# A hybrid mixer and expert block on one Trainium2 core: running sums of the decays through DRAM, tokens first in stage 1

## The chip, the core and the metric

The program runs on one core of one Trainium2 chip. The core has five engines with a queue of instructions each: TensorE (PE in the views), VectorE (DVE), ScalarE (ACT), GpSimd (POOL) and SyncE (SP, which here only issues transfers), and 16 DMA engines. The engines wait for one another on semaphores only. The metric is device time in microseconds of one execution: the median of three runs.

## What is computed

One block over 256 tokens of width 1024, float32 throughout: a modulated norm, a hybrid mixer (a gated delta rule, "gdn", with 8 heads, beside a state-space part, "ssd", with 16 heads), and a mixture of 32 experts; then a second block of other kind. The change touches the head of the first mixer:

```
mod = silu(c) @ ada_w + ada_b                      # six rows of 1024
h = rmsnorm(x, norm1_g) * (1 + sc1) + sh1
proj = h @ w_in                                    # qkv and gate of gdn; gate, xbc and dt of ssd
qkv = silu(causal_dwconv(gdn_qkv)); q, k = l2norm(q) * DK**-0.5, l2norm(k)
g  = -exp(gdn_a_log) * softplus(gdn_a + gdn_dt_bias)     # log decays, gdn
xbc = silu(causal_dwconv(ssd_xbc) + conv_b)
a  = -exp(ssd_a_log) * softplus(ssd_dt + ssd_dt_bias)    # log decays, ssd
gam = cumsum(g); a_cum = cumsum(a)                 # over the tokens of a chunk
decay = exp(gam[l] - gam[s]) for s <= l, per head  # the same for a_cum
```

Both parts need, for every head and every pair of tokens, the difference of two running sums. The kernel has tokens on the 128 partitions, in two halves (T = 2), so the sum of token l is a column (one value per partition) and that of token s a row that must stand on all partitions.

## The kernel before

Each `with nc.Block()` is a stage: all engines meet at its end, and within it each engine's code is an order written out by hand. The first four hold the first mixer.

*Stage 1* (L331 to L552): SP loads `c`, `ada_b` and `norm1_g` as rows, the tokens `x_res`, and through a ring of six slots of 2 MB the chunks of `ada_w` and `w_in` (`Ring.add`, `Ring.load`, `Ring.take`: a chunk's load waits for the semaphore that its slot's last user raises). TensorE multiplies the condition with four chunks of `ada_w` (L299, `modulation_sums`), ScalarE copies the result (L479), and `spread` (L398) brings it to columns. ScalarE squares the tokens (L489), takes the root (L491), VectorE scales the tokens (L523), TensorE transposes them (L420), and VectorE applies shift and scale feature block by feature block (L538, `s_hk`). Then TensorE computes the 12 projection units of `xbc` (L406, `half_unit`, four feature blocks of eight at a time), VectorE runs the convolution of each unit (L322, L324: four instructions), TensorE the narrow products (L454: the decays' inputs) and the ssd gates (L463).

*Stage 2* (L604 to L842): 24 units of gdn projection (L629, 8 products each) from six chunks of `w_in`, each with VectorE's convolution (L320, L324) and ScalarE's silu (L736). PSUM has three banks for units: unit u waits until the convolution of unit u - 3 is done. Between the units lies the ssd part for half t at units 0, 3, 5, 9 (and 12 on): `decay_rows` (L653) multiplies the decays, repeated by ScalarE along the free dimension (L708), with the triangle `tri_le`, which gives the running sums as rows on all partitions; VectorE's `pair_exponents` (L781) subtracts the column and writes `dmat`; ScalarE exponentiates (L717). `lengths(b)` (L639) sums squares of q and k for the norm and waits for ScalarE's copy of the one before (L754). At the end TensorE computes four gdn gates (L701).

*Stage 3* (L1202 to L1740): the chunked delta rule. ScalarE repeats the gdn decays (L1485); TensorE's `decay_rows` (L1258) and `decay_columns` (L1263) put the differences in PSUM; ScalarE takes the absolute value (L1491) and exponentiates (L1493); VectorE's `lower` (L1571) makes the triangular matrix, GpSimd masks it (L1227), and the inverse is built in levels (L1331, L1347, L1353), beside which modulation chunks, the output projection and their loads run. SP loads `mods` (`ada_b` on all partitions, L1207) here. At its end the first expert weights are loaded as slots come free.

*After it*: the first experts stream 32 sets of weights from DRAM through eight slots (L1805, L1832), each load waiting for the product that frees its slot; then the second mixer and second experts.

## Time and profile before

| | us |
|---|---|
| median of three runs | 2095.73 (2095.64 to 2097.11) |
| profiled execution | 2094.25 |
| its span | 2092.5 |
| TensorE busy in the span | 1936.1 (93%) |
| VectorE, ScalarE, GpSimd busy | 499.9, 325.9, 81.9 |
| DMA | 707.29 MB, 338 GB/s over the span |

The span runs from the first to the last instruction of the profiled execution; the rest of its time lies around it. TensorE's matmuls are pipelined and float32 ones leave two records each; "busy" includes the tail of each group. "idle before" is the time in which the engine had nothing to run ahead of a row, with what ended it. PEclk is the granted TensorE clock, as a share of full speed.

### The profile page before, as it was taken

How to read it: one execution, taken by the hardware profiler on the slowest of the kernel's cores; microseconds unless marked ns; L12 is line 12 of the kernel's file. 1: busy time of each engine (PE TensorE's matmuls, PEld its weight loads, DVE VectorE, ACT ScalarE, POOL GpSimd, SP SyncE). 2: the span in 40 equal slices, each digit the busy share in tenths (PEclk: the TensorE clock that was granted, in tenths of full speed). 3: DMA queues.
4: the chain of work that ended last, by engine and by line, in shares of the span. 5: the costliest groups of instructions: out<-in, count | busy, mean ns of one | idle time of the engine just before them, and what ended most of it. 6: DMA issues, size and time to landing. Idle time of an engine off the chain costs nothing. (4 is left out here: it accounts for less than half of the span.)

```text
span 2092.5 us, 24721 instructions
## 1 busy us (share of the span) xinstructions
PE 1936.1 (93%) x10246; PEld 907.1 (43%) x10246; DVE 499.9 (24%) x1040; ACT 325.9 (16%) x580; POOL 81.9 (4%) x185
## 2 busy tenths in 40 slices
PE   6999999989999999999999999999999887877877
PEld 4687665543333333333333333445454432322332
DVE  1456444422222122121112221232342200000000
ACT  2234421210000000000000000124341100000001
POOL 2010031000000000000000000000020000000000
PEclk9999999999999999999999999999999999999999
DMA  9333157599999999999999999955255799999996
GB/s 339 128 131 108 62 208 291 218 374 421 428 428 428 428 428 428 429 428 429 429 428 429 428 429 428 407 166 174 64 201 205 331 425 428 427 429 428 429 428 273
DMA packets 99150, 707.29 MB, mean 338 GB/s; under 512 B 12378, under 2 KB 17996, under 8 KB 61836
## 3 DMA queue, kind: packets, MB, share of 16 engines
q1 hardware_dynamic: 99084, 706.36, 82.1%
q8 instruction: 47, 0.77, 0.1%
q14 instruction: 19, 0.16, 0.0%
HBM read 705.29 MB, written 1.05 MB: 338 GB/s over the span
## 5 line engine op out<-in xcount | busy, mean ns | idle before, releaser
L1805 PE MATMUL ps<-ring,arena 128*64 128x512 f32 x1536 | 337.9, 593 | 11.2 <-DMA ring<-in_moe_w_gu 11.2
L3049 PE MATMUL ps<-ring,arena 128*32 128x512 f32 x768 | 176.8, 630 | 46.6 <-DMA ring<-in_w_up 24.1
L1805 PEld LDWEIGHTS ps<-ring,arena 128*64 128x64 f32 x1536 | 109.9, 137 | 233.0 <-issue 206.7
L1832 PE MATMUL ps<-ring,arena 128*64 128x512 f32 x768 | 170.2, 592 | 0.0
L2265 PE MATMUL ps<-ring 128*128 128x512 f32 (+1 forms) x320 | 138.6, 583 | 0.7 <-ACT ring L2658 0.6
L1862 ACT ACTIVATE arena<-arena 128x512 f32<-128x512 f32 x32 | 20.1, 630 | 758.3 <-DVE arena L1893 758.3
L3049 PEld LDWEIGHTS ps<-ring,arena 128*32 128x32 f32 x768 | 52.0, 115 | 170.5 <-issue 166.7
L1805 PE MATMUL ps<-arena 128*64 128x512 f32 x512 | 114.0, 593 | 4.1 <-DMA arena<-in_moe_w_gu 4.1
L1168 PEld LDWEIGHTS ps<-arena 128*128 128x128 f32 x832 | 100.1, 198 | 35.3 <-issue 32.7
L1168 PE MATMUL ps<-arena 128*128 128x128 f32 x832 | 108.1, 287 | 2.3 <-DVE arena L1160 1.3
L1832 PEld LDWEIGHTS ps<-ring,arena 128*64 128x64 f32 x768 | 54.9, 137 | 109.9 <-issue 96.1
L1893 DVE TENSOR_SCALAR arena<-ps 128x512 f32<-128x512 f32 x32 | 22.1, 692 | 316.3 <-PE ps L1805 316.3
L2265 PEld LDWEIGHTS ps<-ring 128*128 128x128 f32 x320 | 59.3, 191 | 66.5 <-issue 64.1
L629 PE MATMUL ps<-arena,ring 128*128 128x256 f32 x384 | 85.1, 379 | 1.0 <-PEq L331 1.0
L629 PEld LDWEIGHTS ps<-arena,ring 128*128 128x128 f32 x384 | 72.7, 190 | 15.3 <-issue 6.1
L1904 DVE TENSOR_TENSOR arena<-ps,arena 128x512 f32<-128x512 f32 x32 | 22.1, 692 | 237.2 <-PE ps L1832 237.2
L3070 PE MATMUL ps<-ring,arena 128*32 128x512 f32 x384 | 63.4, 652 | 13.7 <-DMA ring<-in_w_down 13.7
L1805 PEld LDWEIGHTS ps<-arena 128*64 128x64 f32 x512 | 36.3, 137 | 78.6 <-issue 69.2
L3049 PE MATMUL ps<-arena 128*32 128x512 f32 x256 | 56.5, 593 | 13.6 <-DMA arena<-in_w_up 7.2
L3122 DVE TENSOR_TENSOR arena<-arena 128x256 f32<-128x256 f32 x8 | 3.4, 426 | 271.2 <-PE ps L3049 271.2
L1776 PE MATMUL ps<-arena 64*128 64x512 f32 x264 | 65.6, 615 | 0.9 <-DVE arena L1904 0.9
L1794 PE MATMUL ps<-arena,masks 128*64 128x512 f32 x256 | 60.4, 592 | 1.3 <-issue 1.3
(608 smaller groups left out, 1980.9 us busy)
## 6 DMA issues: line engine op xcount, KB each, us to landing
ring<-in_moe_w_gu SPq DMA_DIRECT2D x96, 2048.0 KB, 28.0
ring<-in_moe_w_down SPq DMA_DIRECT2D x48, 2048.0 KB, 30.2
arena<-in_moe_w_gu SPq DMA_DIRECT2D x31, 2048.0 KB, 26.7
ring<-in_w_gate SPq DMA_DIRECT2D x26, 2048.0 KB, 26.9
ring<-in_w_down SPq DMA_DIRECT2D x24, 2048.0 KB, 27.1
ring<-in_w_in SPq DMA_DIRECT2D x22, 2048.0 KB, 8.5
ring<-in_w_up SPq DMA_DIRECT2D x22, 2048.0 KB, 24.1
arena<-in_moe_w_down SPq DMA_DIRECT2D x16, 2048.0 KB, 32.2
```

The costliest lines, as they stand in the source:

```text
L629: last = M.matmul(ps[:, u % GB, 0:T * P], w[:, k, c * P:(c + 1) * P], hT[:, k, :], start=(k == 0), stop=(k == KD - 1))
L1168: last = M.matmul(ps[:, bank, k4 * P:(k4 + 1) * P], x_tok[:, t, k * P:(k + 1) * P], onehot[:, t, :], start=(t == 0), stop=(t == T - 1))
L1776: last = M.matmul(ps[:, 2 * t + j, :], GT[halves[j], t, :], y2[halves[j], :], start=False, stop=False, skip_group_check=True)
L1794: M.matmul(ps[halves[j], 4 + which, :], bsel[ee][:, 2 * which + j, :], bias_all, start=True, stop=False)
L1805: last = M.matmul(ps[halves[j], 4 + which, :], xgT[buf][:, k, CAP * ee:CAP * ee + CAP], w[k2][:, at:at + 512], start=False, stop=(k == KD ...
L1832: last = M.matmul(ps[halves[j], 6, :], yT[:, k % KH, halves[k // KH]], w[k % KH][:, 512 * j:512 * j + 512], start=False, stop=(k == 2 * KH ...
L1862: A.activation(sg, tg, ACT.Sigmoid, scale=1.702).then_inc(s_sig, 1)
L1893: V.tensor_scalar(tg, ps[:, 4, :], 7.0, None, ALU.min).then_inc(s_g, 1)
L1904: V.tensor_tensor(y2, ps[:, 6, :], g2s, ALU.mult).then_inc(s_y2, 1)
L2265: last = M.matmul(ps[:, bank, 0:n], uT[:, k, t * P:(t + 1) * P], w[:, k, :], start=(k == 0), stop=(k == KD - 1))
L3049: last = M.matmul(ps[quads[e], 4 + which, :], xgT[:, k, quads[e]], w[e][k], start=(k == 0), stop=(k == KD - 1))
L3070: last = M.matmul(ps[quads[e], (4, 7)[d], :], yT[:, k, quads[e]], w[e][k][:, 512 * d:512 * (d + 1)], start=(k == 0), stop=(k == KH - 1))
```

## The change

Four things are changed.

1. *Running sums through DRAM.* TensorE multiplies the decays of all 24 heads (8 gdn, 16 ssd) with `tri_le` once per half, which gives the sums with heads on 24 partitions; ScalarE copies them; SP stores them to a DRAM tensor `decay_sums` and loads them back repeated on all 128 partitions: `abc` for the ssd part (again for the second half once the products have read it), `gbc` for the gdn part. `decay_rows` of both stages, `decay_columns` of stage 3 and ScalarE's repeats go. VectorE's `pair_exponents` of the first eight heads stands at units 2 and 14 instead of 0 and 12. In stage 3 ScalarE computes the absolute differences itself, head by head.
2. *Lengths one unit later*: `lengths` at even units 6 to 20 instead of odd units 5 to 19.
3. *Tokens first in stage 1*: `x` is loaded first; the raw tokens are transposed; the root factors are spread over partitions by a product with a diagonal and multiplied in as VectorE takes the transposes from PSUM.
4. *`xbc` weights by rows*: four chunks of 256 rows by 1536 columns in place of three of 1024 by 512, and the 12 units take feature blocks 0 to 3 first, all of them, then 4 to 7. The ring then holds one chunk more; two `load` calls move with it, and the wait of the `n2g` load goes.

```diff
-        ra.add(cols(w_in, C_XBC + 512 * j), (KD, 512), (s_unit, 4 * j + 4), (4, 5, 0)[j])
+        ra.add(w_in[2 * P * j:2 * P * j + 2 * P, C_XBC:C_XBC + 12 * P].rearrange("(k p) n -> p k n", p=P), (2, 12 * P),
+               (s_rows_done, 1) if j < 2 else (s_unit, 12), (1, 2, 0, 3)[j])
...
+            sp.dma_start(x_res, a["x"][0].rearrange("(t p) d -> p t d", p=P)).then_inc(s_x, 16)
             sp.dma_start(rowsC[0:8, :], a["c"][0].rearrange("(c p) -> c p", p=P)).then_inc(s_rowc, 16)
             sp.dma_start(rowsC[8:24, :], a["ada_b"][0][0:2 * D].rearrange("(c p) -> c p", p=P)).then_inc(s_rowc, 16)
             sp.dma_start(rowsC[24:32, :], a["norm1_g"][0].rearrange("(c p) -> c p", p=P)).then_inc(s_rowc, 16)
-            ra.load(sp, 1)
-            sp.dma_start(x_res, a["x"][0].rearrange("(t p) d -> p t d", p=P)).then_inc(s_x, 16)
             ra.load(sp, 4)
             sp.dma_start(rowsA[0:96, :], a["gdn_conv_w"][0].rearrange("k (c p) -> (k c) p", p=P)).then_inc(s_rows, 16)
             sp.dma_start(rowsB[0:48, :], a["ssd_conv_w"][0].rearrange("k (c p) -> (k c) p", p=P)).then_inc(s_rows, 16)
             sp.dma_start(rowsB[48:60, :], a["ssd_conv_b"][0].rearrange("(c p) -> c p", p=P)).then_inc(s_rows, 16)
-            ra.load(sp, 7)
+            ra.load(sp, 8)
...
+            def unit_rows(u, w, j):
+                for k in range(2 * j, 2 * j + 2):
                     if u == 0:
                         pe.wait_ge(s_hk, k + 1)
-                    last = M.matmul(unit_bank(u), w[:, k, (u % 4) * P:(u % 4 + 1) * P], hT[:, k, :], start=(k == 0 and not 4 <= u < 8),
+                    last = M.matmul(unit_bank(u), w[:, k % 2, u * P:(u + 1) * P], hT[:, k, :], start=(k == 0 and u < 6),
                                     stop=(k == KD - 1), skip_group_check=True)
-                if half:
-                    last.then_inc(s_unit, 1)
+                return last
...
             pe.wait_ge(s_const, 1)
+            pe.wait_ge(s_x, 16)
+            tokens(0)
             pe.wait_ge(s_rowc, 48)
             M.transpose(ps[:, 7, 0:32], rowsC[0:32, :], ident[0:32, 0:32]).then_inc(s_first, 1)
+            tokens(1).then_inc(s_first, 1)
             pe.wait_ge(s_cw, 1)
             modulation_sums(pe, cond, 4)
+            pe.wait_ge(s_dg, 1)
+            for t in range(T):
+                last = M.matmul(ps[:, 6, t * P:(t + 1) * P], ones[:, :], root_diag[:, t, :])
+            last.then_inc(s_rsp, 1)
             spread(0)
-            for t in range(T):
-                pe.wait_ge(s_h, t + 1)
-                for k in range(KD):
-                    last = M.transpose(ps[:, k // 2, (k % 2) * 256 + t * P:(k % 2) * 256 + (t + 1) * P],
-                                       hn[:, t, k * P:(k + 1) * P], ident[:, :])
-            last.then_inc(s_first, 1)
             modulation_sums(pe, cond, 5)
             spread(1)
             w = [ra.take(pe), None]
-            pe.wait_ge(s_xh, 2)
-            for u in range(8):
-                if u == 2:
+            for u in range(4):
+                unit_rows(u, w[0], 0)
+            w[1] = ra.take(pe)
+            for u in range(4):
+                unit_rows(u, w[1], 1)
+            pe.wait_ge(s_rtk, 1)
+            pe.wait_ge(s_rows, 48)
+            M.transpose(ps[:, 6, 0:96], rowsA[0:96, :], ident[0:96, 0:96])
+            M.transpose(ps[:, 6, 96:156], rowsB[0:60, :], ident[0:60, 0:60]).then_inc(s_first, 1)
+            for u in range(4, 12):
+                for j in range(2):
+                    last = unit_rows(u, w[j], j)
+                if u == 5:
+                    pe.wait_ge(s_cw, 2)
+                    modulation_sums(pe, cond, 6)
+                if u == 6:
                     pe.wait_ge(s_hk, 4)
-                if u == 4:
-                    pe.wait_ge(s_rows, 48)
-                    M.transpose(ps[:, 7, 64:160], rowsA[0:96, :], ident[0:96, 0:96])
-                    M.transpose(ps[:, 7, 160:220], rowsB[0:60, :], ident[0:60, 0:60]).then_inc(s_first, 1)
-                    w[1] = ra.take(pe)
-                half_unit(u, w[u // 4], 0)
-                if u == 6:
-                    modulation_sums(pe, cond, 4)
-            spread(2)
-            modulation_sums(pe, cond, 5)
-            spread(3)
-            for u in range(8):
-                if u >= 4:
-                    pe.wait_ge(s_conv, u - 3)
-                half_unit(u, w[u // 4], 1)
-            pe.wait_ge(s_cw, 3)
-            w = ra.take(pe)
-            for u in range(8, 12):
-                half_unit(u, w, 0)
-                half_unit(u, w, 1)
+                    spread(2)
+                if u == 8:
+                    modulation_sums(pe, cond, 6)
+                if u == 9:
+                    spread(3)
+            last.then_inc(s_rows_done, 1)
+            w = [ra.take(pe), ra.take(pe)]
+            for u in range(12):
+                if u >= 6:
+                    pe.wait_ge(s_conv, u - 5)
+                for j in range(2):
+                    last = unit_rows(u, w[j], 2 + j)
+                last.then_inc(s_unit, 1)
...
+            dve.wait_ge(s_const, 1)
+            vv(V.tensor_scalar(root_diag[:, 0, :], ident[:, :], rstd[:, 0:1], None, ALU.mult))
+            V.tensor_scalar(root_diag[:, 1, :], ident[:, :], rstd[:, 1:2], None, ALU.mult).then_inc(s_dg, 1)
+            dve.wait_ge(s_first, 2)
+            dve.wait_ge(s_rtk, 1)
+            for j in range(4):
+                vv(V.tensor_tensor(hT[:, 2 * j:2 * j + 2, :], ps[:, j, :].rearrange("p (k n) -> p k n", k=2), rep(roots, 2), ALU.mult))
...
+            def repeat_decays(t):
+                sp.dma_start(abc, row_everywhere(kept_sums[8:24, t * P:(t + 1) * P])).then_inc(s_abc, 16)
+
+            sp.wait_ge(s_hst, 1)
+            sp.dma_start(kept_sums, head_sums).then_inc(s_hsd, 16)
+            sp.wait_ge(s_hsd, 16)
+            repeat_decays(0)
             sp.dma_start(sng, row_everywhere(a["ssd_norm_g"][0])).then_inc(s_p3, 16)
-            ra.load(sp, 17)
+            for t in range(T):
+                sp.dma_start(gbc[t], row_everywhere(kept_sums[0:8, t * P:(t + 1) * P])).then_inc(s_gbc, 16)
+            ra.load(sp, 15)
+            sp.wait_ge(s_y3, 1)
+            repeat_decays(1)
+            ra.load(sp, 18)
...
-            def decay_rows(t, q):
-                if q == 0:
-                    pe.wait_ge(s_abc, t + 1)
-                    if t:
-                        pe.wait_ge(s_y3t, 1)
-                        pe.wait_ge(s_st, 1)
-                    M.matmul(ps[:, 4, 0:SH], tri_le[:, :], dec[:, t, 8:24])
-                    M.matmul(ps[:, 4, 16:16 + SH], ones[:, :], dec[:, t, 8:24])
-                else:
-                    pe.wait_ge(s_dx, 3 * t + 2)
-                for h in range(8):
-                    last = M.matmul(ps[:, 6 + h // 4, (h % 4) * P:(h % 4 + 1) * P], abc[:, 8 * q + h, :], tri_le[:, :])
-                last.then_inc(s_row, 1)
+            def sums_by_head():
+                for t in range(T):
+                    last = M.matmul(ps[0:24, 7, t * P:(t + 1) * P], dec[:, t, :], tri_le[:, :])
+                last.then_inc(s_hs, 1)
+
+            def decay_columns(t):
+                if t:
+                    pe.wait_ge(s_y3t, 1)
+                    pe.wait_ge(s_st, 1)
+                M.matmul(ps[:, 4, 0:SH], tri_le[:, :], dec[:, t, 8:24])
+                M.matmul(ps[:, 4, 16:16 + SH], ones[:, :], dec[:, t, 8:24]).then_inc(s_row, 1)
...
+            sums_by_head()
             for u in range(24):
                 if u % 4 == 0:
                     w = ra.take(pe)
                 gdn_unit(u, w)
                 t = u // 12
                 if u in (0, 12):
-                    decay_rows(t, 0)
+                    decay_columns(t)
                     group_products(t)
-                if u in (3, 15):
-                    decay_rows(t, 1)
                 if u in (5, 17):
                     value_transposes(t)
                 if u in (9, 21):
                     products(t)
-                if u >= 5 and u % 2 == 1 and u <= 19:
-                    lengths((u - 5) // 2)
+                if u >= 6 and u % 2 == 0 and u <= 20:
+                    lengths((u - 6) // 2)
...
+            act.wait_ge(s_hs, 1)
+            A.activation(head_sums, ps[0:24, 7, 0:T * P], ACT.Copy).then_inc(s_hst, 1)
...
             def pair_exponents(t, q):
-                dve.wait_ge(s_row, 2 * t + q + 1)
-                if q == 0:
-                    vv(V.tensor_copy(acum, ps[:, 4, 0:SH]))
-                    V.tensor_tensor(edec, ps[:, 4, 16:16 + SH], acum, ALU.subtract).then_inc(s_dx, 1)
+                dve.wait_ge(s_abc, 16 * t + 16)
                 for h in range(8):
-                    ins = V.scalar_tensor_tensor(dmat[:, 8 * q + h, :], ps[:, 6 + h // 4, (h % 4) * P:(h % 4 + 1) * P],
+                    ins = V.scalar_tensor_tensor(dmat[:, 8 * q + h, :], abc[:, 8 * q + h, :],
                                                  acum[:, 8 * q + h:8 * q + h + 1], neg_u, ALU.subtract, ALU.add)
...
             ra.load(sp, 20)
             sp.dma_start(mods.rearrange("p a b -> p (a b)"), row_everywhere(a["ada_b"][0][2 * D:6 * D])).then_inc(s_p6, 16)
             sp.dma_start(rb, row_everywhere(a["router_b"][0])).then_inc(s_n2, 16)
-            sp.wait_ge(s_grow, 1)
             sp.dma_start(n2g, row_everywhere(a["norm2_g"][0])).then_inc(s_n2, 16)
...
-            pe.wait_ge(s_gbc, 1)
-            decay_rows(0, 0)
-            decay_columns(0, 0)
             per_head(2, lambda h: (qkvT[:, 8 + h, toks(0)], qkvT[:, 8 + h, toks(0)])).then_inc(s_gkk, 1)
             pe.wait_ge(s_gx, 1)
             transpose_heads(6, 8, 0).then_inc(s_kT, 1)
...
+            def differences(t):
+                act.wait_ge(s_gbc, 16 * t + 16)
+                for h in range(GH):
+                    last = A.activation(Q1[t][:, h, :], gbc[t][:, h, :], ACT.Abs, bias=gam[:, t, h:h + 1], scale=-1.0)
+                last.then_inc(s_ab, 1)
+                act.wait_ge(s_ab, t + 1)
+                A.activation(Q1[t], Q1[t], ACT.Exp, scale=-1.0).then_inc(s_E, 1)
+
             act.wait_ge(s_gx, 1)
+            differences(0)
```

How the order of instructions moves, at three places. The rows name line, operation, output and inputs; `arena`, `ring`, `small` and `ps` are the program's SBUF and PSUM areas.

TensorE at the start of stage 1, before:

```order
L413 MATMUL ps<-ident,arena 128x32
L299 MATMUL ps<-ring,cond 32x512 x8
L398 MATMUL ps<-ones,arena 128x1 x4
L420 MATMUL ps<-ident,arena 128x128 x16
L299 MATMUL ps<-ring,cond 32x512 x8
L398 MATMUL ps<-ones,arena 128x1 x4
L406 MATMUL ps<-arena,ring 128x256 x16
```

and now:

```order
L414 MATMUL ps<-ident,arena 128x128 x8
L422 MATMUL ps<-ident,arena 128x32
L414 MATMUL ps<-ident,arena 128x128 x8
L302 MATMUL ps<-ring,cond 32x512 x8
L428 MATMUL ps<-arena,ones 128x128 x2
L400 MATMUL ps<-ones,arena 128x1 x4
L302 MATMUL ps<-ring,cond 32x512 x8
L400 MATMUL ps<-ones,arena 128x1 x4
L408 MATMUL ps<-arena,ring 128x256 x16
```

The 16 transposes stand ahead of the first modulation sums, and two root products are new.

TensorE at the start of stage 2, before:

```order
L629 MATMUL ps<-arena,ring 128x256 x8
L648 MATMUL ps<-small,tri_le 128x16
L649 MATMUL ps<-small,ones 128x16
L653 MATMUL ps<-tri_le,ring 128x128 x8
L658 MATMUL ps<-arena 128x128 x2
L660 MATMUL ps<-ident,arena 128x128 x2
L629 MATMUL ps<-arena,ring 128x256 x24
L653 MATMUL ps<-tri_le,ring 128x128 x8
```

and now:

```order
L675 MATMUL ps<-tri_le,small 24x128 x2
L660 MATMUL ps<-arena,ring 128x256 x8
L682 MATMUL ps<-small,tri_le 128x16
L683 MATMUL ps<-small,ones 128x16
L687 MATMUL ps<-arena 128x128 x2
L689 MATMUL ps<-ident,arena 128x128 x2
L660 MATMUL ps<-arena,ring 128x256 x40
```

The sums by head stand ahead of the first unit, and both batches of decay rows are gone.

SP in stage 2, now (before: `sng`, then five chunks of `w_in`):

```order
L630 DMA decay_sums<-arena 24x256 [waits decay_sums_taken]
L627 DMA ring<-decay_sums 128x16x128 [waits decay_sums_stored]
L633 DMA arena<-in_ssd_norm_g 128x1024
L635 DMA ring<-decay_sums 128x8x128 x2
L189 DMA ring<-in_w_in 128x8x512 [waits gdn_projection_ready] x2
L627 DMA ring<-decay_sums 128x16x128 [waits ssd_products_ready]
L189 DMA ring<-in_w_in 128x8x512 [waits gdn_projection_ready] x3
```

The store, its wait and three repeated loads stand ahead of the weights, and the fourth repeated load in their midst.

## Rows read from the trace of the kernel before

**Rows 1.** The page: its head, and what the DMA moved in 40 slices of the span

```profile
span 2092.5 us, 24721 instructions
...
GB/s 339 128 131 108 62 208 291 218 374 421 428 428 428 428 428 428 429 428 429 429 428 429 428 429 428 407 166 174 64 201 205 331 425 428 427 429 428 429 428 273
```

**Rows 2.** Windows at the hand-over; columns: stretch, length, busy us by engine, clock, DMA

```profile
438.00:440.00 2.00, 2.00 (x12) 0.86 (x10) 0.74 (x4) 0.00 (x0) 0.00 (x0) 1.00 0.24 62
```

**Rows 3.** Timeline of TensorE, stage 1: start, us busy, engine line, form, idle before

```profile
10.24 3.64 PE L299 MATMUL ps<-ring,cond 128*32 128x512 f32 x16 [6.67 <-DMA ring<-in_ada_w]
...
19.32 3.53 PE L420 MATMUL ps<-ident,arena 128*128 128x128 f32 x16 [2.80 <-DVE arena L523]
...
22.77 1.92 PE L299 MATMUL ps<-ring,cond 128*32 128x512 f32 x16
...
27.67 7.15 PE L406 MATMUL ps<-arena,ring 128*128 128x256 f32 x32 [1.20 <-DVE arena L538]
...
79.14 1.07 PE L454 MATMUL ps<-arena 128*32 128x256 f32 x16
```

**Rows 4.** Groups of TensorE in stage 2 (109 to 252 us)

```profile
L653 PE MATMUL ps<-tri_le,ring 128*128 128x128 f32 x64 | 8.0, 278 | 0.0
...
L639 PE MATMUL ps<-arena 128*128 128x512 f32 x8 | 4.2, 606 | 2.4 <-ACT arena L754 2.4
```

**Rows 5.** Timelines of stage 3 by engine, ScalarE's 128x128 copy of later, a window

```profile
253.62 0.17 DVE L1589 TENSOR_TENSOR small<-ps,small 128x16 f32<-128x16 f32 x1
...
261.05 2.17 DVE L1571 SCALAR_TENSOR_TENSOR arena<-ps,small,arena 128x128 f32<-128x128 f32 x8 [7.26 <-ACT arena L1493]
...
271.25 2.16 DVE L1571 SCALAR_TENSOR_TENSOR ring<-ps,small,ring 128x128 f32<-128x128 f32 x8 [2.95 <-ACT ring L1505]
...
280.28 0.42 DVE L1621 TENSOR_TENSOR arena<-arena,ps 128x256 f32<-128x256 f32 x1 [1.19 <-PE ps L1353]
...
254.34 1.28 ACT L1487 ACT_TABLE_LOAD   x1
...
259.96 1.06 ACT L1493 ACTIVATE arena<-arena 128x1024 f32<-128x1024 f32 x1
...
418.74 0.28 ACT L1560 ACTIVATE arena<-ps 128x128 f32<-128x128 f32 x1 [0.55 <-PE ps L1456]
...
277.82 1.13 PE L1331 MATMUL ps<-arena 64*64 64x64 f32 x32
...
256.00:258.00 2.00, 2.00 (x4) 0.91 (x4) 0.00 (x0) 0.00 (x0) 0.00 (x0) 0.50 1.04 386
```

**Rows 6.** Timelines: ScalarE's copy of 128x512, VectorE's product of 128x512 from PSUM

```profile
24.77 0.60 ACT L479 ACTIVATE arena<-ps 128x512 f32<-128x512 f32 x1 [0.80 <-PE ps L299]
...
302.82 0.69 DVE L1610 TENSOR_TENSOR arena<-ps,arena 128x512 f32<-128x512 f32 x1 [6.18 <-PE ps L1391]
```

**Rows 7.** Window of stage 1 with the DMA engines full

```profile
6.00:8.00 2.00, 0.00 (x0) 0.00 (x0) 0.00 (x0) 0.00 (x0) 1.71 (x5) 1.00 1.05 410
```

**Rows 8.** Timelines of stage 2: two projection units, ScalarE's copy of lengths

```profile
157.31 7.07 PE L629 MATMUL ps<-arena,ring 128*128 128x256 f32 x32
...
166.19 0.58 ACT L754 ACTIVATE arena<-ps 128x512 f32<-128x512 f32 x1
```

**Rows 9.** Windows of stage 1 before and at the half clock

```profile
46.00:48.00 2.00, 1.28 (x16) 0.40 (x4) 0.00 (x0) 1.03 (x2) 0.00 (x0) 1.00 0.67 70
...
50.00:52.00 2.00, 2.00 (x6) 1.62 (x5) 0.54 (x2) 0.00 (x0) 0.00 (x0) 0.50 1.05 408
```

**Rows 10.** DMA issues: out<-in, engine, count, KB each, us to landing

```profile
arena<-in_w_in SPq DMA_DIRECT2D x2, 64.0 KB, 6.5
...
arena<-in_ada_b SPq DMA_DIRECT2D x1, 2048.0 KB, 19.8
```

**Rows 11.** Groups of VectorE in stage 2

```profile
L781 DVE SCALAR_TENSOR_TENSOR ring<-ps,small,masks 128x128 f32<-128x128 f32 x32 | 8.6, 343 | 0.0
...
L320 DVE TENSOR_SCALAR arena<-ps,convw 128x256 f32<-128x256 f32 x24 | 11.6, 482 | 40.2 <-PE ps L629 40.2
```

138 lines of the change are left out of this document (57 added, 81 removed).

## Prediction

> **What bounds the kernel now.** I read four views in this order: the page, the windows around the hand-over from mixer to experts, the timeline of TensorE in the three stages that the diff touches, and, where TensorE waited, the engine that released it.
>
> The page gives a span of 2092.5 us [rows 1]; the profiled execution took 2094.25 us, 1.75 us around the span, and lies 1.5 us below the median of 2095.73 us. The sum below is taken off that execution and its difference carried to the median.
>
> The first mixer must hand its gain on. From the ninth of 40 slices (418 us on) the DMA engines move 374 and then some 428 GB/s for 18 slices, the expert weights [rows 1], so the length of that part is set by bytes, not by the change. Its start is not: from 438 to 440 us the DMA moved only 62 GB/s [rows 2], because every slot was full and the next load waited for TensorE's first release. All the loads ahead of it wait for the mixer's own steps as well. So what the mixer ends earlier, the stream starts earlier and the kernel ends earlier, one for one. The second mixer and the second experts follow by the same rule and are not edited.
>
> In the first three stages TensorE is nearly always busy. In stage 1 it starts its projection at 27.67 us and reaches the narrow products at 79.14 us [rows 3]. In stage 2 it has one wait of 2.4 us in 142 us [rows 4]. In stage 3 it is held by a chain over ScalarE, VectorE and GpSimd until 277.82 us [rows 5], then is busy again.
>
> **Stage 1, up to the projection (5.9 us).** Before: weights of the first modulation chunk land and TensorE multiplies at 10.24; the raw tokens come next, and ScalarE's squares, the root and VectorE's scaling hold the 16 transposes until 19.32; sums of chunk two follow at 22.77, and the projection at 27.67 [rows 3]. Now the tokens are issued first, at about 0.8 instead of 2.47 us. 1 MB at some 400 GB/s [rows 7] takes 2.6 us, so they land near 6 us and the first chunk about 1 us later than before, at 11.2. The transposes (16, 3.53 us, [rows 3]) are done at 9.8, in time that was empty. Sums one end at 14.8 if they again take 3.64 us; the two root products, ScalarE's copy of sums and of the roots (0.6 each, [rows 6]) give 16.0; four multiplications of 128x512 by VectorE at 0.69 us [rows 6] give 18.9, beside TensorE's spread and second sums (the second chunk lands at 16.6, 5.4 us after the first at 390 GB/s). Sums two end at 19.3, copy 0.6, spread 1.05, shift and scale and the first feature 0.8 to 1.2 [rows 3]: the projection starts at about 21.8. Its first weights, 1.57 MB more, land at 20.6. 27.67 - 21.8 = 5.9 us.
>
> **Stage 1, the projection (2.8 us).** Before, 27.67 to 79.14 is 51.5 us. Its 192 matmul records take 0.216 to 0.218 us each where undisturbed (in stage 2, 32 of them take 7.07 us with the tail of the last, [rows 8]), 41.7 us, with two chunks' sums (1.9 each, as the second in [rows 3]), two spreads (1 each) and 0.4 of parameter transposes between: 47.6 us. The rest is 1.7 us of waits for sums and features, and 1.9 us at half clock: 0.50 granted from 50 to 52 us, after a stretch with TensorE idle a third of the time [rows 9]. The new order puts units' work between sums and spread, so the 1.7 us go. The clock fall follows that idle stretch and may go too; I take half, 1.0. Weights now come by rows, so the second half of every unit comes at the end: 12 units of 1.73 us on TensorE against 2.0 us of convolution by VectorE. VectorE lags by some 5 us at its end, not 2; TensorE waits only for unit 7 onward's bank and for the ninth convolution before the narrow products, which is done 1 us in time. The gate's first weights now wait for `s_rows_done` (near 50 us) and land at 58, needed at 71: hidden. Together 8.7 us for stage 1.
>
> **Stage 2 (9.4 us).** 32 decay products of 128x128, 64 records in four batches, go: 8.0 us busy with their tails [rows 4], 7.3 us from start to start of what follows. Two products of 24x128 come, 0.4 us by the same price. TensorE is the bound, so 6.9 us are won whole. The 2.4 us wait is that of lengths for ScalarE's copy of the ones before, which stood behind its squares, root and table loads and ran at 166.19 [rows 8]. One unit later (3.5 us) the copy is long done, and ScalarE also loses the repeat of the decays: 2.4 won.
>
> What is added is a round trip: ScalarE's copy, a store of 24 KB, a wait, and a load of 1 MB in 2048 pieces of 512 B. SP then also delays `sng` and later weights by some 10 us, which nobody needs before ten units on. The nearest rows of small pieces are two loads of 64 KB in 1024 pieces of 64 B, 6.5 us to landing each [rows 10]. The store stands behind the last 2 MB of projection weights, still in flight at stage start until 6.6 us in. Then 0.4 to issue, 2 to start and land, and the transfer: 2.6 us by the rate of [rows 7], at most 8 by twice the small loads' excess. So `abc` lands 12 to 17 us into the stage. VectorE asks for it after its third convolution, at 14. Behind that wait stand eight 0.34 us instructions [rows 11] and the fourth convolution, for which TensorE's sixth unit waits at 19: `abc` may land at 14.7 for nothing, and every us later costs one. VectorE was idle 40 us for TensorE in this stage [rows 11], so the rest is covered. I take zero, with 2.5 as the dear end. In the second half the reload starts at unit 9 and is needed at unit 14, 20 us later: free.
>
> The 2.6 us rest on loads of 2 to 4 KB pieces, which ran at 410 GB/s [rows 7]. The Trainium skill, DMA: Bandwidth & Descriptors, section Bandwidth, gives 6.15 us for 1 MB (341 GB/s), and its Specifications want at least 512 B per piece for line rate, which these just reach; by that `abc` would land at 15.2 and the sum would lose 0.5 us. No row here shows 512 B pieces in such number.
>
> **Stage 3 (5.5 us).** 32 records of rows, 8 of 128x512 columns and ScalarE's two 1 us repeats leave the head of the chain. Before, the first exponentials are ready when VectorE starts at 261.05 [rows 5]. Now, from VectorE's column sums (done at 253.8): eight differences at 0.28, a table load 1.28, the exponential 1.06 [rows 5]: 258.4, 2.6 earlier. For the second half, VectorE's rest of the first (kx, queries, values: 3 x 1.2) ends at 264.5 and TensorE's key products 1.9 after the queries, 265.2; ScalarE's second differences are ready at 264.6. So VectorE's second eight start near 265.7, against 271.25 [rows 5]: 5.5 us, and the first level product at 272.3 instead of 277.82. The half clock of 256 to 258 [rows 5] stretched the column products; it now falls on work with slack. The load into `mods` (2 MB of `ada_b`) landed 19.8 us after its issue at 258.7 [rows 10], at 278.5, and VectorE first needs it at 280.28 [rows 5]. With the need 5.5 us earlier this would be late; but the load of `w_out` that stood ahead of it now stands behind, 2 MB or 5.4 us, so it keeps its 1.7 us of slack, and `w_out` itself is needed 15 us later. Bounds: 2.6 (first half alone) to 7 (VectorE's second eight start at 264.6, when their differences are ready).
>
> **Sum.** 8.7 + 9.4 + 5.5 = 23.6 us off: 2070.7 for the profiled execution, 2072 on the median. The low ends are 2.8 in stage 1 (nothing ahead of the projection), 6.9 in stage 2 (9.4 less 2.5), 2.6 in stage 3: 12 us off, 2083. The high ends are 11.3 in stage 1 (sums one in 1.92 us as later ones, and the whole 1.9 of the clock), 9.4 and 7: 28 off, 2068.
>
> **The rivals.** *The front is bound by the order of loads* (0.17): the tokens ahead push modulation and projection weights back by 2.6 us, and TensorE finds its weights late; stage 1 then wins 2.8 at its waits and nothing ahead: 17.7 off, 2078. For it: DMA is full from 4 to 44 us. Against: weights landed before they were asked for, except the first.
> *More half clock* (0.10): TensorE still idles before its projection, and its first 8 us run at half the granted clock (1.2 of 2.4 GHz): 4 us back and none of the 1.0: 18.6 off, 2077. For it: transposes at 19.32 took twice their later price.
> The Trainium skill, TensorE: Matmul & The Clock Gate, part 1, says that the clock halves after idling and returns after sustained work. The trace agrees: 0.50 granted behind the stretch with 1.28 of 2 us busy [rows 9]. By that rule the case above would give 2077, and the forecast's closed gaps the whole 1.9 us, 2071.
> *The expert stream swallows the gain* (0.04): if the slots were filled no earlier, no change, 2095. Against: 62 GB/s before 440 us.
> *The round trip ends late and it is slower* (0.04): VectorE stands before its fourth convolution, all TensorE units behind. The mechanism decides from a landing of `abc` at 14.7 + 23.6 = 38 us into the stage; at 43, 5 us over, 2100. That needs 30 us for 1 MB; nothing in [rows 10] comes near.
> *More than 28 us off* (0.03): the stage starts, each some 1 us after the last matmul, are also quieter.
>
> **How the numbers follow.** The forecast has 0.62: 2072. The range holds it with its unknown costs and the first two rivals, 2066 to 2082. A measurement can tell about 0.2% (4.2 us) from no change. Faster: 0.62 + 0.17 + 0.10 + 0.03 = 0.92; same 0.04; slower 0.04.
>
> **What would show it.** Projection starts at 21 to 23 us; narrow products at 70; no TensorE wait at lengths in stage 2, no VectorE wait for DMA at `dmat` over 1 us, stage 2 shorter by 9; first level product 20 us into stage 3 instead of 25.5; the expert stream full from about 417 us; end of the mixer earlier by the same as the whole. Wrong if a wait for `decay_sums` appears above 3 us, or if the DMA does not pause before the expert stream.

## The result, and the profile after

The changed kernel takes 2075.61 us (median of 4 runs, 2075.49 to 2076.23), the kernel before, in runs on the same chip, 2095.68 us (2095.39 to 2097.11): 20.1 us less, a ratio of 0.9905 with a 95% interval of 0.9892 to 0.9917. The forecast was 23.6 us off, 2072. The profiled execution took 2075.69 us, its span is 18.5 us shorter than that of before, whose profiled execution lay 1.4 us under its median.

The page of the changed kernel, to be read beside [rows 1]:

```profile
span 2074.0 us, 24556 instructions
...
GB/s 310 174 184 118 167 212 206 292 393 420 428 427 428 428 428 428 430 427 428 429 429 427 428 429 429 394 126 176 83 215 208 330 426 428 428 428 428 428 428 272
```

In the eighth of the 40 slices the DMA engines now move 292 GB/s instead of 218, in the ninth 393 instead of 374, and the plateau is the same 428: the expert stream starts earlier and runs no faster. The pause ahead of it is still there: from 420 to 422 us the DMA moves 5 GB/s, where [rows 2] has 62 from 438 to 440. From the first expert products to the end of the span it took 1657.5 us, before 1657.0.

Stage 1, timeline of TensorE in the changed kernel, against [rows 3]:

```profile
6.15 1.94 PE L414 MATMUL ps<-ident,arena 128*128 128x128 f32 x8 [6.15 <-DMA arena<-in_x]
...
11.57 3.24 PE L302 MATMUL ps<-ring,cond 128*32 128x512 f32 x16 [1.34 <-DMA ring<-in_ada_w]
...
16.88 1.92 PE L302 MATMUL ps<-ring,cond 128*32 128x512 f32 x16 [0.30 <-DMA ring<-in_ada_w]
...
21.66 8.55 PE L408 MATMUL ps<-arena,ring 128*128 128x256 f32 x32 [1.09 <-DVE arena L550]
...
71.05 1.07 PE L468 MATMUL ps<-arena 128*32 128x256 f32 x16
```

Windows of the same stage (stretch, length, busy us of PE, PEld, DVE, ACT, POOL with counts, clock, DMA share, GB/s):

```profile
22.00:24.00 2.00, 2.00 (x6) 1.53 (x6) 0.49 (x2) 0.00 (x0) 0.00 (x0) 0.50 1.01 393
24.00:26.00 2.00, 2.00 (x10) 1.72 (x9) 0.00 (x0) 0.00 (x0) 0.00 (x0) 0.87 1.04 361
```

The projection starts 6.0 us earlier and the narrow products come 8.1 us earlier. The projection itself went from 51.5 to 49.4 us. The half clock of before went, but the projection's first products now run under one: 32 records take 8.55 us where 7.07 is the undisturbed price, and no later window of the projection shows one.

Stage 2, groups of TensorE from 101.2 us to the stage's end, against [rows 4]. The 64 records of decay products are gone and nothing waits at the lengths:

```profile
L660 PE MATMUL ps<-arena,ring 128*128 128x256 f32 x384 | 85.3, 379 | 0.0
...
L670 PE MATMUL ps<-arena 128*128 128x512 f32 x8 | 4.1, 592 | 0.0
L670 PE MATMUL ps<-arena,ones 128*128 128x512 f32 x8 | 4.1, 592 | 0.0
```

The new round trip, first the timeline of the queue that issues loads:

```profile
102.22 0.33 SPq L630 DMA_DIRECT2D decay_sums<-arena  x1
108.55 0.37 SPq L627 DMA_DIRECT2D ring<-decay_sums  x1
```

The timeline of VectorE where it takes the loaded rows:

```profile
115.52 2.54 DVE L809 SCALAR_TENSOR_TENSOR ring<-ring,small,masks 128x128 f32<-128x128 f32 x8
```

And the load as a row of the DMA issues (count, KB each, us from issue to landing):

```profile
ring<-decay_sums SPq DMA_DIRECT2D x1, 1024.0 KB, 6.1
```

The stage starts at 101.19 and lasts 133.50 us, before 109.28 and 143.06: 9.56 us won. The store waits behind the last projection weights and the load, which waits for it, is issued 6.3 us after it; the load lands near 114.6, 13.5 us into the stage, and VectorE takes it at 115.52 with no wait.

Stage 3, timeline of TensorE, against [rows 5]:

```profile
234.69 0.36 PE L1299 MATMUL ps<-small,tri_le 128*128 128x8 f32 x2 [0.94 <-PEq L623]
...
240.10 1.04 PE L1288 MATMUL ps<-ident,arena 128*128 128x128 f32 x8
246.59 3.57 PE L1283 MATMUL ps<-arena 128*128 128x128 f32 x16 [5.45 <-DVE arena L1586]
...
256.84 1.13 PE L1335 MATMUL ps<-arena 64*64 64x64 f32 x32
```

The timeline of VectorE there:

```profile
241.02 2.16 DVE L1573 SCALAR_TENSOR_TENSOR arena<-ps,small,arena 128x128 f32<-128x128 f32 x8 [4.88 <-ACT arena L1494]
...
244.23 1.05 DVE L1596 TENSOR_TENSOR small<-small 128x8 f32<-128x8 f32 x1
...
250.27 2.16 DVE L1573 SCALAR_TENSOR_TENSOR ring<-ps,small,ring 128x128 f32<-128x128 f32 x8 [2.00 <-PE ps L1283]
```

The stage starts 17.65 us earlier (234.69 against 252.34). The first level product comes 22.15 us into it, before 25.48: 3.3 us, not 5.5. TensorE now stands idle 5.45 us for VectorE's queries, and the key products behind that take 3.57 us, where the same 16 records of the first half take 2.03, in stretches with a granted clock of 0.60 and 0.55.

### The profile page after: what moved, and what is told of

Same layout as the page of the kernel before. It is cut to its first block and busy times, and to the rows that moved or that the text cites. A ratio compares the mean times of both kernels' runs of the same rounds, so it can differ in the third digit from the quotient of the medians.

```text
span 2074.0 us, 24556 instructions
## 1 busy us (share of the span) xinstructions
PE 1924.3 (93%) x10150; PEld 896.2 (43%) x10150; DVE 502.1 (24%) x1044; ACT 327.7 (16%) x593; POOL 82.2 (4%) x185
```

## Experiments

Each median stands beside runs of the kernel before on the same chip (2095.73, 2096.12 and 2095.82 us for the three groups of four). The runs of one kernel spread over up to 6.6 us and the ratios' intervals are some 2.7 us wide to each side, so what is worth 1 or 2 us is read from stage lengths in the profiles, and the medians only have to agree.

**1. Stage 1 alone.** The kernel before with the diff's first stage, and one load more in each later count, since the projection's weights are now four loads.

> The kernel before with the change's first stage alone: tokens first, transposed raw, their roots multiplied in on VectorE, projection weights by rows. Stages 2 and 3 are those of the kernel before. Theory (each stage hands its gain on): narrow products at 71.0 us instead of 79.1, whole kernel 8.1 us shorter, 2087.6 against 2095.7, stages 2 and 3 as long as before (143.1 us, first level product 25.5 us into its stage). Rival (the expert stream or a later wait takes part of it): less than 6 us. If stage 1 is worth only its waits, 2.8 us, the narrow products come at 76.

Measured: 2087.29 us, 8.4 off, ratio 0.9968 (0.9956 to 0.998). In the profile stages 2 and 3 are those of before (143.07 us in stage 2). But this profile's front, timeline of TensorE, was slower than that of the changed kernel:

```profile
12.15 3.64 PE L302 MATMUL ps<-ring,cond 128*32 128x512 f32 x16 [2.00 <-DMA ring<-in_ada_w]
...
18.37 3.37 PE L302 MATMUL ps<-ring,cond 128*32 128x512 f32 x16
...
24.61 7.75 PE L408 MATMUL ps<-arena,ring 128*128 128x256 f32 x27 [1.10 <-DVE arena L550]
```

Both chunks' sums at nearly twice the 1.92 us price put the projection at 24.61, so this execution won 4.9 us at the narrow products, not 8.1. It was all the same the shortest of the six runs of this kernel (2086.87 us, 7.4 under the profiled execution of before): 1.7 of the 7.4 us came in stage 3, whose code is that of before (experiment 2 says why), and 1.6 from the first expert products on. So the whole kernel's time agrees with the forecast for the stage within its interval (4.2 to 9.2 us off), but it is no clean measure of the stage. Eight profiles here have this front and this projection; their narrow products come between 71.05 and 74.28 us, 4.9 to 8.1 before those of the kernel before and 6.6 on the average. The kernel before has one profile, so how much its own front varies stays open.

**2. Stages 1 and 2, stage 3 as before.**

> The changed kernel with the third stage of the kernel before (decay differences by TensorE's products and ScalarE's repeats; the two loads for that stage are left out). Theory: 8.1 + 9.5 = 17.6 us shorter than before, 2078.1; stage 2 lasts 133.5 us instead of 143.1, without a TensorE wait at the lengths; first level product 25.5 us into stage 3 again. Beside the changed kernel it is some 2 to 3 us longer, since the trace gave stage 3 only 3.3 us of the 5.5 forecast, of which 0.5 or so went missing later. Rival (stage 3's change was worth its 5.5 us, and something else in the same trace was slow): 2081.

Measured: 2076.45 us, 19.3 off, ratio 0.991 (0.9897 to 0.9924). Stage 2 is as short as in the changed kernel. And stage 3, unchanged code, reached its first level product 23.82 us in, in experiment 1 too, not 25.48. Timeline of TensorE:

```profile
236.69 2.05 PE L1284 MATMUL ps<-tri_le,arena 128*128 128x128 f32 x16
238.58 1.89 PE L1289 MATMUL ps<-small,tri_le 128*128 128x512 f32 x4
...
259.42 1.13 PE L1357 MATMUL ps<-arena 64*64 64x64 f32 x32
```

In the profiled execution of before, the products in these two places took 2.68 and 2.97 us, across the 0.50 window of [rows 5]. Of three executions of this code one had that fall of the clock, and 1.7 of the 3.3 us are its absence. The stage's own change is worth 23.82 - 22.15 = 1.7 us in this pair of profiles, and 0.7 to 1.8 over all eight that have the changed stage (22.03 to 23.17 us to the first level product); the medians, 2076.45 against 2075.61 and 2076.53 for the changed kernel, cannot show it. The theory had 2 to 3 us here, and both it and its rival were too high.

**3. Unread products in the front's last gaps.** Behind the second chunk's sums `fill(4)`, behind its spread `fill(5)`:

```diff
+            def fill(n):
+                for i in range(n):
+                    M.matmul(ps[:, 4, 0:256], ident[:, :], x_res[:, 0, 0:256])
```

> The changed kernel with 9 products of 128x256 that nobody reads, put in TensorE's two gaps ahead of the projection (4 behind the second chunk's sums, 5 behind its spread). Theory (the half clock granted from 22 to 24 us follows from TensorE's near idle 18 to 22 us): granted clock above 0.9 from 20 to 26 us, the first 32 projection products in 7.1 us instead of 8.6, narrow products 1 to 1.5 us earlier, kernel 1 to 1.5 us shorter than the changed one. Rival 1 (those first records are slow for their weights, which land in the same microseconds): clock better but no time won. Rival 2 (idling before 16 us decides, not the last gaps): half clock as before, and 0.2 us lost to the added products.

Measured: 2075.68 us (0.9893 to 0.992). The projection ran undisturbed, 32 records in 7.07 us and 47.91 us in all, close to the 47.6 that the prediction counted without any half clock. Timeline of TensorE:

```profile
26.24 7.07 PE L408 MATMUL ps<-arena,ring 128*128 128x256 f32 x32
```

But the second sums had taken 3.43 us in this execution, the 18 added records took 2.0 and 2.4 us, over twice the gaps, and the projection started at 26.24. With the last two gaps filled the half clock is gone, and 1.5 us with it, as the theory has it; experiment 10 shows that those two gaps alone do not bring it. The fill was too long to gain from it.

**4. Unread products ahead of the late key products.**

```diff
+            pe.wait_ge(s_L, 1)
+            for i in range(24):
+                M.matmul(cell(2, i % 8), qkvT[:, 8, toks(1)], qkvT[:, 8, toks(1)])
             pe.wait_ge(s_qk, 1)
```

> The changed kernel with 24 products of 128x128 that nobody reads, put in stage 3 ahead of the second half's key products, in the 5.45 us in which TensorE waits for VectorE (they start when the first lower triangles are done, near 243.1 us, into the two banks those leave). Theory (the key products ran at half clock for that idling): key products 2.0 us instead of 3.57, second lower triangles 1.5 us earlier, first level product 20.6 us into the stage instead of 22.15, kernel 1.5 us shorter than the changed one. Rival (2 us of idling suffice for the fall, so the fill itself runs at half clock, lasts 6 us and holds the key products): same or up to 2 us slower than the changed kernel.

Measured: 2077.34 us (0.9901 to 0.9928), first level product at 24.26 us into the stage. Timeline of TensorE:

```profile
243.53 7.25 PE L1309 MATMUL ps<-arena 128*128 128x128 f32 x48 [2.10 <-DVE arena L1576]
250.62 1.95 PE L1283 MATMUL ps<-arena 128*128 128x128 f32 x16
```

The rival held: 2.1 us of idling is followed by slow records here too (granted clock 0.50 from 244 to 246 us), the fill paid part of the slow price itself, and behind it the key products ran in 1.95 us. That their 3.57 us was the clock's doing is shown. That filling cannot cure it is not: from 248 to 250 us, at full clock, 20 records of the fill ran in 2 us, so its 48 need an estimated 5 us even then, and only 3.4 lie between its start and the place where the key products start in the changed kernel. No run has a shorter fill here.

**5. The changed kernel once more.**

> The changed kernel itself once more, for runs beside the three kernels sent with it and for a second profile. Theory (the profiled executions of one kernel differ in where the clock falls): stage 2 again 133.0 to 133.5 us, stage 3 to its first level product again 22.15 us with TensorE idle 5.45 us and key products at 3.6 us, since both are set by the program; the projection start between 21.7 and 24.6 us, where the four profiles so far lie. Rival (the slow key products were a chance of one execution): they take 2.0 us here.

Measured: 2076.53 us (0.9895 to 0.9926). The theory held: stage 2 is 133.50 us again, and stage 3 repeats with 22.35 us to the first level product, idle 5.45, key products 3.78 us. The front does not repeat: the first sums took the fast 1.92 us, ended early, TensorE then idled 1.63 us for the second chunk, and that chunk's sums took 3.43 us. Timeline of TensorE:

```profile
11.52 1.92 PE L302 MATMUL ps<-ring,cond 128*32 128x512 f32 x16 [1.58 <-DMA ring<-in_ada_w]
...
16.83 3.43 PE L302 MATMUL ps<-ring,cond 128*32 128x512 f32 x16 [1.63 <-DMA ring<-in_ada_w]
...
23.13 8.83 PE L408 MATMUL ps<-arena,ring 128*128 128x256 f32 x32 [1.09 <-DVE arena L550]
```

**6. Key products in other banks.** They go where the first lower triangles leave room, and the keys' transposes where they stood:

```diff
-            pe.wait_ge(s_qk, 1)
-            per_head(4, lambda h: (qkvT[:, 8 + h, toks(1)], qkvT[:, 8 + h, toks(1)])).then_inc(s_gkk, 1)
-            pe.wait_ge(s_Ut, 1)
-            transpose_heads(0, 16, 1).then_inc(s_vT, 1)
-            pe.wait_ge(s_L, 1)
-            transpose_heads(2, 8, 1).then_inc(s_kT, 1)
+            pe.wait_ge(s_L, 1)
+            per_head(2, lambda h: (qkvT[:, 8 + h, toks(1)], qkvT[:, 8 + h, toks(1)])).then_inc(s_gkk, 1)
+            pe.wait_ge(s_qk, 1)
+            transpose_heads(4, 8, 1).then_inc(s_kT, 1)
+            pe.wait_ge(s_Ut, 1)
+            transpose_heads(0, 16, 1).then_inc(s_vT, 1)
```

The second half's lower triangles, keys and inverse then read banks 2, 4 and 2 in place of 4, 2 and 4.

> The changed kernel with the second half's key products of stage 3 in the two banks that the first lower triangles leave (free near 243 us), and its keys' transposes in the two banks that the first queries leave, so the key products no longer wait for VectorE's queries. Theory (that wait and the half clock behind it hold the second lower triangles): key products start near 243.2 us instead of 246.6 and end at 245.2 to 246.8 even at half clock; second lower triangles start at 248.3 instead of 250.3, when VectorE has done its rest of the first half; first level product 20.2 us into the stage instead of 22.15, kernel 2 us shorter than the changed one. Rival (ScalarE's second differences, ready at 247.3, or VectorE's work behind sets the time): under 0.5 us.

Measured: first level product 20.07 us into the stage, 2.1 to 2.3 sooner than in both profiles of the changed kernel. The key products start behind 2.1 us of idling instead of 5.45, still slow, but done before VectorE wants them, which now runs on without a gap. Timeline of TensorE:

```profile
246.18 3.68 PE L1283 MATMUL ps<-arena 128*128 128x128 f32 x16 [2.10 <-DVE arena L1573]
```

Its timeline of VectorE:

```profile
250.54 0.68 DVE L1578 TENSOR_TENSOR arena<-masks,arena 128x512 f32<-128x512 f32 x1
251.14 2.15 DVE L1573 SCALAR_TENSOR_TENSOR ring<-ps,small,ring 128x128 f32<-128x128 f32 x8
```

The median, 2076.25 us (0.9895 to 0.9922; runs from 2073.06 to 2079.65), does not show it: this profile's front started its projection at 24.34. By the stage the theory holds, by the median it stays open.

**7. Small products in all of the front's idle times, first dose.**

```diff
+            fill(8, P)
             pe.wait_ge(s_x, 16)
             tokens(0)
...
             tokens(1).then_inc(s_first, 1)
+            fill(6, P)
```

and one and two of 128x256 behind the second sums and their spread.

> The changed kernel with small products nobody reads in TensorE's idle times of the front: 8 of 128x128 ahead of the tokens, 6 behind their transposes, one of 128x256 behind the second chunk's sums and two behind its spread, shorter than the 9 tried before, which kept the clock up but stood 2 us in the way. Theory: transposes 2.0 us instead of 3.9, first sums 1.9 instead of 3.2 to 3.6, projection start 21.7 us with no half clock behind it, narrow products at 69.5, kernel 1.5 to 2 us shorter than the changed one. Rival (they do not suffice for the clock and stand in the way): the same or up to 1 us longer.

Measured: 2075.31 us (0.9891 to 0.9922). The transposes took 1.18 and 1.09 us instead of 1.94 and 1.97, and the projection 47.98 us. In between TensorE still idled 2.03 us before the first chunk, the clock was granted at 0.50 from 14 to 18 us, the second sums took 3.30 us and the projection started at 23.16. Half of the theory: what it expects where the gaps are closed, not where they were left.

**8. The repeated load issued late,** behind the norm weights and the two loads for stage 3.

> The changed kernel with the first repeated load of the decays issued behind the norm weights and the two loads for stage 3, 1.5 MB of row-by-row loads: it lands some 22 to 24 us into stage 2 instead of 13.3. Theory (as forecast: VectorE stands in front of its fourth convolution for it and TensorE behind, each us past 14.7 costs one): VectorE waits 7 to 9 us for it and the kernel is 7 to 9 us longer than the changed one, 2083 to 2085. Rival (TensorE's lead over VectorE and VectorE's idle time take it up): under 3 us.

Measured: 2078.22 us (0.9903 to 0.993), stage 2 134.61 us, 1.1 more than in the changed kernel. VectorE waited 5.65 us for the load, and TensorE only 0.75 us for VectorE. Timeline of VectorE:

```profile
121.50 2.19 DVE L809 SCALAR_TENSOR_TENSOR ring<-ring,small,masks 128x128 f32<-128x128 f32 x8 [5.65 <-DMA ring<-decay_sums]
```

Timeline of TensorE:

```profile
125.69 3.72 PE L660 MATMUL ps<-arena,ring 128*128 128x256 f32 x16 [0.75 <-DVE arena L327]
```

The rival held. The price of "one us for every us past 14.7" was wrong: of 5.7 us later (VectorE starts 20.06 instead of 14.33 us into the stage), 5.4 of them past 14.7, 1.1 reached the end. TensorE has three banks and runs ahead; it is its seventh unit, behind the values' transposes and 23.3 us into the stage, that waits for the fourth convolution, not the sixth at 19.

**9. Weights by columns, tokens first.** Three loads of 512 columns again, eight first halves of units, chunks three and four, eight second halves, four whole units.

> The changed kernel with its tokens first, but the projection's weights by columns and its units in halves, in the order of the kernel before (eight first halves, with the third and fourth modulation chunks between and behind, then the second halves). Theory (the order by rows won the 1.7 us of waits that the kernel before had inside its projection): from projection start to narrow products 51 to 51.5 us instead of 49.4 to 49.7, start itself 21.7 to 24.6 as in the other profiles, kernel 1.5 to 2 us longer than the changed one. Rival (order by rows won nothing, the shorter projection is VectorE's and the banks' doing): 49.5 us here too.

Measured: 2079.52 us, ratio 0.9927 (0.9913 to 0.9941), 3 to 4 us over the changed kernel. From projection start to narrow products 52.75 us, against 49.4 to 49.7. The start waits for its larger first load, and two waits stand inside again. Timeline of TensorE:

```profile
22.35 10.10 PE L406 MATMUL ps<-arena,ring 128*128 128x256 f32 x32 [1.73 <-DMA ring<-in_w_in]
...
45.25 1.05 PE L398 MATMUL ps<-ones,arena 128*128 128x1 f32 x8 [0.72 <-ACT arena L487]
47.28 27.89 PE L406 MATMUL ps<-arena,ring 128*128 128x256 f32 x128 [0.97 <-DVE arena L543]
```

The order by rows is worth those 1.7 us inside, as counted, and 0.6 at the start, which was not: its first load is 1.5 MB instead of 2. The rest of the 3.2 us between the two projections is a longer slow stretch at its head, 10.10 us for 32 records instead of 8.55 to 8.83.

**10. Tokens behind the first chunk.**

> The changed kernel with the tokens' load issued behind the first modulation chunk, as before the change; TensorE's order stays, transposes first. Theory (tokens first is what moves the projection's start): tokens land near 11.5 us, transposes end at 13.5 to 15.4, first sums at 15.4 to 17, projection starts at 24 to 26.5 us instead of 21.7 to 24.3, kernel 2 to 3 us longer than the changed one. Rival (the second chunk of weights sets the start, so the order of the first two loads is free): start as in the changed kernel, no loss.

Measured: 2076.75 us (0.9901 to 0.9928). The tokens land at 12.99, the sums start at 17.00 and 21.25, the projection at 26.04, 1.4 to 4.4 us later than in the eight profiles of the changed front. Timeline of TensorE:

```profile
23.89 1.05 PE L401 MATMUL ps<-ones,arena 128*128 128x1 f32 x8 [0.72 <-ACT arena L495]
26.04 7.14 PE L409 MATMUL ps<-arena,ring 128*128 128x256 f32 x32 [1.10 <-DVE arena L551]
```

The projection runs in 47.98 us with no half clock, so the narrow products come at 74.02, within the 71.05 to 74.28 of those eight profiles. The order of the first two loads moves the projection's start, as the theory says; that it is worth 2 to 3 us in the end neither the profile nor the medians show.

This settles something about the clock as well. The two gaps ahead of the projection are those of the changed kernel (0.72 and 1.09 us), and in all eight profiles of that kernel's front a half clock follows them (8.55 to 8.83 us for 32 records). Here none does, nor in the kernel before, where the projection starts with 7.15 us behind gaps of 0.7 and 1.20 us [rows 3]. So these two gaps alone do not bring the fall, though filling them removes it (experiment 3). TensorE's work ahead of them differs: in the eight it idles 1.3 to 2.3 us between transposes and first sums, while here the transposes and both batches of sums follow one another closely, and in the kernel before it idles 2.80 us ahead of its transposes. What decides it stays open.

**11. The lengths back where they were.**

```diff
-                if u >= 6 and u % 2 == 0 and u <= 20:
-                    lengths((u - 6) // 2)
+                if u >= 5 and u % 2 == 1 and u <= 19:
+                    lengths((u - 5) // 2)
```

> The changed kernel with the lengths back at units 5, 7, 9 and so on. In the kernel before TensorE waited 2.4 us for one of them, and ScalarE has since lost its repeats of the decays. Theory (ScalarE's copy of the lengths before ends at 154.8 in the trace of the changed kernel, and the lengths asked for one unit earlier would come at 154.1): a wait of 0.7 us, stage 2 133.7 us, kernel 0.7 us longer. Rival 1 (the loss of the repeat took nothing away; squares and root held it): the whole 2.4 us returns, stage 2 135.4. Rival 2: no wait at all, 133.0.

Measured: 2085.49 us, ratio 0.9948 (0.9934 to 0.9961), 9 to 10 us over the changed kernel and more than any theory gave. Timeline of TensorE in stage 2:

```profile
157.91 1.12 PE L670 MATMUL ps<-arena 128*128 128x512 f32 x2 [2.44 <-ACT arena L780]
158.87 3.62 PE L660 MATMUL ps<-arena,ring 128*128 128x256 f32 x16
...
178.06 2.08 PE L670 MATMUL ps<-arena,ones 128*128 128x512 f32 x2 [2.77 <-ACT arena L780]
179.93 9.23 PE L660 MATMUL ps<-arena,ring 128*128 128x256 f32 x32
```

ScalarE around the third wait:

```profile
174.45 1.28 ACT L742 ACT_TABLE_LOAD   x1
176.46 1.06 ACT L742 ACTIVATE ring<-ring 128x1024 f32<-128x1024 f32 x1 [0.73 <-DVE ring L809]
177.43 0.58 ACT L780 ACTIVATE arena<-ps 128x512 f32<-128x512 f32 x1
```

The old 2.44 us wait returns whole, so the lost repeats on ScalarE had taken nothing off it. A second long one appears: the decay exponentials of the second half now sit two units later (unit 14 instead of 12), and the copy of the lengths stands behind a table load and the exponential. Behind it the clock is granted at 0.50 from 178 to 184 us, and 32 projection records take 9.23 instead of 7.07 us. Stage 2 lasts 142.8 us: nearly all that the stage had won is gone, 5.4 of the 9.3 us by waits and 3.2 by the slow records. No run has the exponentials back at unit 12, so how much of the loss is due to their move is read from this trace alone.

**12. Both repairs together:** the banks of experiment 6, and the fill of 7 with 12 products behind the transposes and 3 of 128x256 behind the first spread.

> The changed kernel with both edits that the traces asked for: stage 3's key products in the banks left by the first lower triangles, and unread products in the front's idle times, now more of them (8 ahead of the tokens, 12 behind their transposes, 3 of 128x256 behind the first spread, 1 and 2 behind the second sums and spread). Theory: no half clock between 8 and 28 us, both chunks' sums in 1.9 us, projection start at 21.7, narrow products at 69.7, first level product 20.1 us into stage 3: 1.5 to 3 us in the front and 2.1 in stage 3, so 2072 to 2073 where the changed kernel runs at 2075.6 to 2076.5. Rival (expert stream or later clock falls take it): 2075 to 2076.

Measured: 2071.16 us (runs from 2070.3 to 2071.94), ratio to before 0.9883 (0.9868 to 0.9898): 24.7 us off, where the changed kernel had 20.1 and 19.6 beside its own runs of before. The medians lie 4.5 and 5.4 us apart and the runs do not meet, though the changed kernel itself was not run beside this one. Timeline of TensorE:

```profile
11.92 1.92 PE L302 MATMUL ps<-ring,cond 128*32 128x512 f32 x16 [0.81 <-DMA ring<-in_ada_w]
...
17.23 1.93 PE L302 MATMUL ps<-ring,cond 128*32 128x512 f32 x16 [0.22 <-DMA ring<-in_ada_w]
...
22.01 7.54 PE L408 MATMUL ps<-arena,ring 128*128 128x256 f32 x32
```

The granted clock reads 1.00 in each stretch from 12 to 28 us, both sums take 1.9 us, the projection's first 32 records 7.54, the narrow products come at 70.39 and the first level product 20.07 us into stage 3. From there to the first expert products it took 157.97 us, where the profiles of the changed kernel have 159.6 and 159.8; experiment 7, with the changed kernel's stage 3, took 157.83, so this belongs to the execution and not to the edit. It is the fastest version here. The profile gives 0.7 to 2.4 us to the front and 2.1 to 2.3 to stage 3. Which edit gives what the medians show stays open: each repair alone left the median at 2076.25 and 2075.31, and the fill here is also larger than in experiment 7.

## Why the prediction came out as it did

It said 2072 by 8.7 + 9.4 + 5.5 us; 20.1 came, inside the range, with two terms too high and one cause misnamed. By the profiles it is 8.1 + 9.6 + 3.3 = 21.0, less 1.9 in the rest of stage 3 and 0.5 behind it, 18.5; the profiled execution of before lay 1.4 us under its median and that of the changed kernel at it, which makes the 20.1. Part of the agreement is luck: stage 1's 8.1 is the best of eight profiles, and stage 3's 3.3 holds 1.7 us of a clock fall that only the profile of before had. Some terms are also added up 0.1 to 0.3 us wrong: the undisturbed projection's terms give 47.9 us and not 47.6, 1.7 and 1.0 give 2.7 and not 2.8, and 6.9 and 2.4 give 9.3 and not 9.4.

**Up to the projection (5.9): right, where the clock allows.** 6.0 in the changed kernel's profile. Eight profiles of this front have the projection at 21.66, 21.68, 21.74, 22.30, 23.13, 23.58, 24.34 and 24.61 us. The forecast took one start for granted where it hangs on how long the first products run slow. By experiment 10, 1.4 to 4.4 us of it come from the order of the first loads; the start there is still 1.6 us before that of the kernel before.

**The projection (2.8): 2.1, and 1.8 to 1.9 in the other seven profiles.** The 1.7 us of waits went, by the order by rows (experiment 9). The 1.0 us for the clock did not come: the step that failed is "the clock fall follows that idle stretch and may go too". That stretch went, and a new fall of nearly the same size came at the projection's head, in all eight profiles. Where the gaps of 0.7 and 1.1 us ahead of the projection are filled, it starts at full clock (experiments 3, 7 and 12); but experiment 10 has the same gaps and no fall, so what else it takes stays open. The rival "more half clock" had this mechanism right and its price too high: 1.5 to 1.8 us, not 4. Without any fall the projection took 47.91 and 47.98 us, as the terms add up.

**Stage 2 (9.4): 9.56, right in size, half right in cause.** The wait for the lengths went because they are asked for later, and not because ScalarE lost its repeats. And the 6.9 us are "won whole" only with that shift: in experiment 11 the removal without it, with the second half's exponentials two units later, leaves 0.3 of the 9.6 us in stage 2 (143.06 to 142.78).

**The round trip (0): right.** It landed 13.5 us into the stage, forecast 12 to 17; and the price past 14.7 was wrong, 1.1 us for 5.4 (experiment 8), so it is safer than the prediction had it. The Trainium skill, DMA: Bandwidth & Descriptors, section Bandwidth, was weighed with 6.15 us for the transfer of 1 MB; with the prediction's 2 us to start and land that makes an estimate of 8.2 from issue to landing. By the 410 GB/s of the rows it is 4.6, and 6.1 was measured, between the two.

**Stage 3 (5.5): 3.3 in the profile, 0.7 to 1.8 by the code.** Two steps failed. The base was one execution with a clock fall of 1.7 us in it (experiments 1 and 2, the same code without it), and the prediction dismissed that fall as landing "on work with slack". And "key products 1.9 after the queries" is 3.57, behind a wait of 5.45 us for those queries, and 3.4 to 3.8 in each of the eight profiles with that wait; the 1.05 us of `beg` on VectorE's path was not counted either. Second lower triangles were forecast 13.4 us into the stage and came at 15.58: 1.6 of the 2.2 us are the clock.

**One for one (right).** The span is 18.5 us shorter, the first level product came 21.0 us and the first expert products 19.0 us earlier. The 2 us between went in stage 3's rest: from the first level product to the first expert products 159.6 us instead of 157.7. That varies with the execution: the fourteen profiles here have 157.7 to 159.8, and experiments 4 and 7, with the changed kernel's code there, 158.1 and 157.8. Seven of them show a stall of 0.9 to 1.3 us that the profile puts down to issue, and take 158.5 us or more; the changed kernel's first profile is one of the seven (1.16 us). What decides it stays open. From the first expert products to the end of the span, profiles of all kernels here have 1655 to 1658 us, whatever the front did.

## What to carry to other kernels

A term that is read from one profiled execution carries that execution's clock: ask of each row whether its mean is the usual one before using it as a base, and of each gap that the change opens or leaves on TensorE what the products behind it will cost. When the busiest engine loses work, look at who it will wait for next and move that request in the same edit; here the shift of the lengths held nearly all of stage 2's gain. Removing the wait in front of a gap (other banks) won 2.1 us in its stage; unread products in a gap can pay only where they fit into time that is idle anyway, so count them at the price of the clock that they will find.
